# Seven block products instead of eight for 23 pairs of value slabs a layer in a PEER down projection (one core, Trainium2)

## The chip, the cores and the metric

One core of one Trainium2 chip runs the whole kernel. The metric is the time of one execution on the device, in microseconds; lower is better. Names of engines are those of the profile: PE is TensorE (PEld its weight loads), DVE VectorE, ACT ScalarE, POOL GpSimd, SP the queue from which the slabs are fetched.

## What is computed

Two layers of a hybrid decoder over 264 token rows (256 prompt tokens and 8 samples) of width D = 1024. Each layer ends in a PEER feed-forward over 16384 experts, and the change lies in the last part of it, in which the experts' values are summed up:

```python
h = jax.nn.gelu(jnp.einsum('td,ted->te', xb, u_tab[eidx]).astype(F32))
w = (gates * h).astype(xb.dtype)
return jnp.einsum('te,ted->td', w, v_tab[eidx])
```

The kernel computes it densely for the 256 prompt tokens: w is a matrix of 256 tokens by 16384 experts that is zero where an expert was not chosen, and the output is w times the value table of 16384 by 1024, in float32. A layer norm of `alpha * x + output` follows.

## The kernel before, in words

**The stage.** `peer_down` walks through the value table in 128 slabs of 128 experts by 1024 columns (512 KB each). Slab n is multiplied by the block `big[:, n, 0:256]` (128 experts by 256 tokens, the gated activations, which lie in SBUF). There are two blocks of 128 tokens (t) and two halves of 512 columns (g), so four block products for each slab, and each of the four has a PSUM bank of its own (bank 2t + g) in which all 128 slabs are summed.

**The split.** To keep float32 precision, each operand is split in two parts of type fp32r: the high part is a copy with the type fp32r (ACT), and the low part is the difference between the float32 value and the high part (DVE). A block product is three matmuls of 128x128 weights by 512 columns: w_hi by v_hi (L2712), w_lo by v_hi (L2713), w_hi by v_lo (L2714). One slab is 12 matmuls.

**Who does what for one slab.** SP fetches it into one of four ring slots (`refill`, L2565) as soon as the low parts of the slab four before are made. ACT makes `w_hi` (256 columns, L2615) and two halves of `v_hi` (512 columns each, L2616), each when PE has finished the half slab that used the same buffer. DVE makes `w_lo` (L2652) and the two halves of `v_lo` (L2656). PE waits for the low parts. There are two buffers for w and four half buffers for v, so the splitting runs one slab ahead of PE. POOL has no arithmetic in the steady part of this stage.

**The order around it.** The first 32 slabs are written out one by one, since other work is woven in there: the values of the samples' experts are gathered and summed in banks 6 and 7 (`values`, L2724), x is transposed into token rows in bank 5 (L2740), and banks 4 and 6 take the samples' sum (L2731). Slabs 32 to 127 run in loops on ACT, DVE and PE. From slab 32 on the banks 4 to 7 are unused. The last two slabs are multiplied one block of tokens at a time, and then `TokenNorm` begins: DVE adds `alpha * x` to the banks (L2834) and the norm follows.

**Elsewhere.** The up projection before this stage and the dense projections split their slabs in the same way, but there POOL makes the low parts (L2150, and L272 in which POOL and DVE take a half each).

Of the kernel before, what the change touches and what calls it, by code (L numbers as in the profile page):

```python
# [23 lines left out]
F32 = mybir.dt.float32  # L24
# [64 lines left out]
class Step:  # L89


    def __init__(self, nc, io, top):
        self.nc, self.io = nc, io
        self.sb = lambda name, shape, dt=F32, ctx=top: ctx.enter_context(nc.sbuf_tensor(name, shape, dt))


        self.ring, self.ring_lo = self.pair("slab_ring", [P, SLOTS, D], "slab_ring_lo", [P, SLOTS, DC, P])
        self.x = self.sb("x_T", [P, DC, T])
        self.const = self.sb("constants", [P, C_END])
        self.ln = self.sb("ln_scale_shift", [P, LAYERS * 3, 2, DC])  # L100
# [8 lines left out]
        self.later = None  # L109
        self.squares, self.slab_hi = self.pair("squares", [P, DC, T], "slab_hi", [P, 2, DC, P])  # L110
# [76 lines left out]
    def slot_free(self, sp, n):  # L187
# [4 lines left out]
        if kind == "projection":  # L192
            sp.wait_ge(self.product_done, k + 1)
        else:
            sp.wait_ge(self.u_product if kind == "u" else self.v_split, 2 * (k + 1))
# [2302 lines left out]
OWN_AT, VALUES_AT, SUM_FROM, UNROLLED = 10, (12, 18), 22, 32  # L2498


def peer_down(step, layer, block, big, row_index, row_gate, ahead, s_read, s_gated, over):
# [4 lines left out]
    vb = step.slabs[base][1]  # L2506
# [15 lines left out]
    norm = TokenNorm(step, layer, z, small, base + NKEYS if layer + 1 < LAYERS else None)  # L2522
    with ExitStack() as c1:

        got = step.sb("gathered_rows" + L, [P, NB, D], ctx=c1)
# [36 lines left out]
        def _(sp):  # L2562
            def refill(i, s):
                sp.wait_ge(step.v_split, 2 * (vb + SLOTS * i + s + 1 - SLOTS))
                sp.dma_start(step.ring[:, s, :], io["v"][layer * P + SLOTS * i + s]).then_inc(step.slab_ready[s], 16)  # L2565
            for s in range(2):
                refill(1, s)
            sp.wait_ge(s_dense, 1)
            sp.dma_start(step.hidden, dense).then_inc(s_out, 16)
            for s in range(2, SLOTS):  # L2570
                refill(1, s)
            with sp.Fori(2, NKEYS // SLOTS) as i:
                for s in range(SLOTS):
                    refill(i, s)
# [5 lines left out]
        def _(pool):  # L2580
# [23 lines left out]
            norm.gpsimd(pool)  # L2604

        @block.scalar
        def _(act):
            def high(i, s, first):
                n = SLOTS * i + s
                act.wait_ge(step.slab_ready[s], 16 * (base // SLOTS + 1) + 16 * i)  # L2610
                for g in range(2):
                    if not (first and s < 2):
                        act.wait_ge(s_y, 2 * n + g - 3)
                    if g:
                        nc.scalar.activation(wh[:, s % 2, :], big[:, n, 0:TP], ACT.Copy).then_inc(s_wh, 1)  # L2615
                    nc.scalar.activation(hi[:, (2 * s + g) % 4, :], step.ring[:, s, g * HALF:(g + 1) * HALF],  # L2616
                                         ACT.Copy).then_inc(s_hi, 1)
            for n in range(1, UNROLLED):
                high(n // SLOTS, n % SLOTS, n < SLOTS)
# [9 lines left out]
                for r in range(6):  # L2629
                    if n == TOKENS_AT[r] + 1:  # L2630
# [3 lines left out]
                        nc.scalar.activation(z[t][:, g * HALF:(g + 1) * HALF], ps[0:b - a, 5, :], ACT.Copy).then_inc(s_xc, 1)  # L2634
                if n == UNROLLED - 2:
# [3 lines left out]
            with act.Fori(UNROLLED // SLOTS, NKEYS // SLOTS) as i:  # L2639
                for s in range(SLOTS):  # L2640
                    high(i, s, False)
# [3 lines left out]
        def _(dve):  # L2645
            def low(i, s):
                n = SLOTS * i + s
                for g in range(2):

                    if g:  # L2650
                        dve.wait_ge(s_wh, n)
                        nc.vector.tensor_tensor(wl[:, s % 2, :], big[:, n, 0:TP], wh[:, s % 2, :].bitcast(F32),  # L2652
                                                ALU.subtract).then_inc(s_wl, 1)
                    dve.wait_ge(s_hi, 2 * n + g - 1)
                    buf = (2 * s + g) % 4
                    nc.vector.tensor_tensor(lo[:, buf, :], step.ring[:, s, g * HALF:(g + 1) * HALF],  # L2656
                                            hi[:, buf, :].bitcast(F32), ALU.subtract).then_inc(step.v_split, 1)

            for n in range(1, UNROLLED):
                low(n // SLOTS, n % SLOTS)  # L2660
# [12 lines left out]
                if n == SUM_FROM + 5:  # L2673
# [4 lines left out]
                    for g in range(2):  # L2678
                        half = z[2][:, g * HALF:(g + 1) * HALF]
                        link(nc.vector.scalar_tensor_tensor(out=half, in0=half, scalar=ALPHA, in1=ps[0:TS, (4, 6)[g], :],  # L2680
                                                            op0=ALU.mult, op1=ALU.add))
# [3 lines left out]
                if n == UNROLLED - 1:  # L2685
# [3 lines left out]
            with dve.Fori(UNROLLED // SLOTS, NKEYS // SLOTS) as i:  # L2689
                for s in range(SLOTS):  # L2690
                    low(i, s)
# [3 lines left out]
        def _(pe):  # L2695
            def down(i, s, first, final):
                n = SLOTS * i + s
                b = s % 2
                if not first:
                    pe.wait_ge(s_wl, n)  # L2700
                for g in range(2):
                    pe.wait_ge(step.v_split, 2 * (vb + n) + g + 1)
                    buf = (2 * s + g) % 4
# [6 lines left out]
                    for t in range(2):  # L2710
# [3 lines left out]
                        last = nc.tensor.matmul(bank, w_hi[:, ts], v_lo, start=False, stop=final)  # L2714
                    last.then_inc(s_y, 1)

# [25 lines left out]
            for n in range(UNROLLED):  # L2742
                down(n // SLOTS, n % SLOTS, n == 0, False)
# [6 lines left out]
            with pe.Fori(UNROLLED // SLOTS, NKEYS // SLOTS - 1) as i:  # L2750
                for s in range(SLOTS):
                    down(i, s, False, False)
            for s in range(SLOTS - 2):
                down(NKEYS // SLOTS - 1, s, False, False)
            for t in range(2):
                for n in (NKEYS - 2, NKEYS - 1):
                    b = n % 2
                    if t == 0:
                        pe.wait_ge(s_wl, n)
                    for g in range(2):  # L2760
                        if t == 0:
                            pe.wait_ge(step.v_split, 2 * (vb + n) + g + 1)
                        buf = (2 * n + g) % 4
# [14 lines left out]
class TokenNorm:  # L2778
# [46 lines left out]
    def vector(self, dve):  # L2825
# [4 lines left out]
        def residual(t):  # L2830
            for g in range(2):
                dve.wait_ge(self.tile_done, 2 * t + g + 1)
                half = z[t][:, self.halves[g]]
                nc.vector.scalar_tensor_tensor(out=half, in0=half, scalar=ALPHA, in1=step.ps[:, 2 * t + g, :], op0=ALU.mult,  # L2834
                                               op1=ALU.add).then_inc(self.sums, 1)
# [119 lines left out]
    def gpsimd(self, pool):  # L2955
# [5 lines left out]
        split_low(step, pool, self.next_slab + 1, (0, 1))  # L2961
        for c in range(DC // 2):
# [121 lines left out]
```

## Time and profile before

| | |
|---|---|
| Time, median of 3 runs | 2197.09 us (2196.4 to 2197.73) |
| The profiled execution's own time | 2196.69 us |
| Its span, first to last instruction | 2194.9 us |
| PE busy, share of the span | 98% |
| DVE / ACT / POOL busy | 77% / 60% / 46% |
| Matmuls of the down stage (L2712 to L2714) | 3 x 1000 recorded |
| Mean rate of HBM traffic | 186 GB/s |

The rows further down come from the one profiled execution. A row of a timeline gives the start in microseconds from the first instruction, the duration, the engine, the line, the operation and output<-input. An `x2` behind it merges two in a row. PE's matmuls are pipelined, so that their recorded durations (0.39 us) overlap, and the distance from one start to the next is what one costs.

### The profile page before, as it was taken

The numbers are of one execution on the slowest core, as the hardware profiler recorded it, in microseconds if no ns is written. First come the engines' busy times: TensorE is split into PE (matmuls) and PEld (weight loads), VectorE is DVE, ScalarE is ACT, GpSimd is POOL, SyncE is SP. The second block draws the span as 40 slices with busy tenths as digits, with TensorE's granted clock in tenths as the row PEclk, the third lists the DMA queues.
The fourth block names the chain that finished last, engine by engine and source line by source line (L and its number), as shares of the span: only waits on it lengthen the run. The fifth ranks groups of instructions, "written<-read, shape, count | busy, mean of one in ns | idle before, by whom it ended". The sixth has DMA issues, their size and how long they took to land.

```text
span 2194.9 us, 45729 instructions
## 1 busy us (share of the span) xinstructions
PE 2154.5 (98%) x15517; PEld 1961.4 (89%) x15517; DVE 1686.1 (77%) x3908; ACT 1316.4 (60%) x3002; POOL 1014.2 (46%) x820
## 2 busy tenths in 40 slices
PE   8989999999999999999999999999999999999998
PEld 8879799999999877888888988999999998788887
DVE  7766489979999856666656656999799996566666
ACT  6544474557777555555566645645777765555555
POOL 6764447997777610000043344589877774000000
PEclk9999999999999999999999999999999999999999
DMA  7548554554444665555545584455444447555554
GB/s 263 161 143 326 206 179 156 171 176 156 155 159 156 206 218 182 193 194 194 193 164 180 191 362 136 166 168 171 167 155 160 156 147 246 195 192 193 194 195 135
DMA packets 112422, 409.32 MB, mean 186 GB/s; under 512 B 16553, under 2 KB 18769, under 8 KB 107089
## 3 DMA queue, kind: packets, MB, share of 16 engines
q1 hardware_dynamic: 107744, 391.45, 52.2%
q0 software_dynamic: 4528, 15.86, 2.3%
q8 instruction: 95, 1.56, 0.3%
q14 instruction: 55, 0.45, 0.1%
HBM read 397.11 MB, written 10.14 MB: 186 GB/s over the span
## 4 chain that ended last, share of the span: by engine, by line
PE 62%; DVE 16%; POOL 7%; issue 4%; ACT 2%; POOLq 0%; ACTq 0%; DVEq 0%
PE banks L2712 10%; PE banks L2714 10%; PE banks L2713 10%; POOL slab_ring_lo L2150 7%; DVE one_hot_gates L2458 7%; PE banks L2201 5%; PE banks L2202 5%; PE banks L2203 5%; PE banks L296 3%; PE banks L297 3%; PE banks L298 3%; DVE slab_ring_lo L272 2%; DVE expert_activations L2475 2%; PE banks L2223 1%; DVE expert_activations L2466 1%
## 5 line engine op out<-in xcount | busy, mean ns | idle before, releaser
L2150 POOL TENSOR_TENSOR slab_ring_lo<-slab_ring,u_hi 128x512 fp32r<-128x512 f32 x504 | 663.1, 1340 | 167.5 <-ACT u_hi L2255 166.7
L2201 PE MATMUL banks<-operand_hi,u_hi 128*128 128x264 f32 x2016 | 584.8, 290 | 1.6 <-POOL slab_ring_lo L2150 1.6
L2203 PE MATMUL banks<-operand_hi,slab_ring_lo 128*128 128x264 f32 x2048 | 583.3, 285 | 0.0
L2202 PE MATMUL banks<-operand_lo,u_hi 128*128 128x264 f32 x2016 | 573.5, 284 | 0.0
L272 POOL TENSOR_TENSOR slab_ring_lo<-slab_ring,slab_hi 128x512 fp32r<-128x512 f32 x162 | 216.5, 1341 | 593.7 <-ACT slab_hi L262 593.0
L2656 DVE TENSOR_TENSOR v_lo<-slab_ring,v_hi 128x512 fp32r<-128x512 f32 x508 | 350.0, 691 | 117.7 <-ACT v_hi L2616 113.0
L2712 PE MATMUL banks<-v_hi,w_hi 128*128 128x512 f32 x1000 | 391.1, 391 | 3.4 <-DVE w_lo L2652 2.2
L2714 PE MATMUL banks<-v_lo,w_hi 128*128 128x512 f32 x1000 | 389.2, 389 | 0.0
L2713 PE MATMUL banks<-v_hi,w_lo 128*128 128x512 f32 x1000 | 389.2, 389 | 0.0
L2255 ACT ACTIVATE u_hi<-slab_ring 128x512 fp32r<-128x512 f32 x504 | 317.7, 631 | 117.8 <-PE banks L2203 115.2
L2203 PEld LDWEIGHTS banks<-operand_hi,slab_ring_lo 128*128 128x128 f32 x2048 | 385.4, 188 | 0.0
L2201 PEld LDWEIGHTS banks<-operand_hi,u_hi 128*128 128x128 f32 x2016 | 380.7, 189 | 3.3 <-POOL slab_ring_lo L2150 2.5
L2202 PEld LDWEIGHTS banks<-operand_lo,u_hi 128*128 128x128 f32 x2016 | 379.6, 188 | 0.0
L2616 ACT ACTIVATE v_hi<-slab_ring 128x512 fp32r<-128x512 f32 x508 | 316.6, 625 | 85.7 <-PE banks L2714 75.9
L2458 DVE TENSOR_SCALAR one_hot_gates<-banks,squares 128x128 f16<-128x128 f32 x1024 | 336.8, 400 | 0.0
L262 ACT ACTIVATE slab_hi<-slab_ring 128x512 fp32r<-128x512 f32 x288 | 174.4, 626 | 129.5 <-PE banks L298 108.2
L2712 PEld LDWEIGHTS banks<-v_hi,w_hi 128*128 128x128 f32 x1000 | 187.7, 188 | 46.8 <-DVE w_lo L2652 6.4
L2714 PEld LDWEIGHTS banks<-v_lo,w_hi 128*128 128x128 f32 x1000 | 187.7, 188 | 39.3
L2713 PEld LDWEIGHTS banks<-v_hi,w_lo 128*128 128x128 f32 x1000 | 187.8, 188 | 38.5
L2615 ACT ACTIVATE w_hi<-expert_activations 128x256 fp32r (+1 forms) x254 | 106.0, 417 | 177.8 <-PE banks L2714 177.2
L2652 DVE TENSOR_TENSOR w_lo<-expert_activations,w_hi 128x256 fp32r<-128x256 f32 x254 | 107.8, 425 | 133.1 <-ACT w_hi L2615 132.4
L272 DVE TENSOR_TENSOR slab_ring_lo<-slab_ring,slab_hi 128x512 fp32r<-128x512 f32 x126 | 125.3, 995 | 98.4 <-ACT slab_hi L262 98.2
(443 smaller groups left out, 3794.1 us busy)
## 6 DMA issues: line engine op xcount, KB each, us to landing
slab_ring<-in_u SPq DMA_DIRECT2D x256, 512.0 KB
slab_ring<-in_v SPq DMA_DIRECT2D x256, 512.0 KB
slab_ring<-in_proj SPq DMA_DIRECT2D x144, 512.0 KB
cache_k_T<-in_cache_k SPq DMA_DIRECT2D x16, 1024.0 KB, 8.7
cache_v<-in_cache_v SPq DMA_DIRECT2D x16, 1024.0 KB, 11.8
memory_T<-in_mem POOLq DMA_DIRECT2D x2, 1024.0 KB, 6.5
sample_state<-in_state POOLq DMA_DIRECT2D x8, 256.0 KB, 3.9
out_mem_k_out<-mem_k_T SPq DMA_DIRECT2D x16, 128.0 KB, 3.0
```

The source lines that it names most:

```text
L272: (nc.gpsimd if engine is nc.gpsimd else nc.vector).tensor_tensor(step.ring_lo[:, n % SLOTS, cs], step.slab(n)[:, cs], step.slab_hi[:, (k ...
L2150: nc.gpsimd.tensor_tensor(step.ring_lo[:, s, g * HC:(g + 1) * HC, :], step.slab(s)[:, g * HC:(g + 1) * HC, :], part[:, buf].bitcast(F32), ...
L2201: nc.tensor.matmul(bank, part[:, buf, k, :], xh[:, c, :], start=(c == 0), stop=False)
L2202: nc.tensor.matmul(bank, part[:, buf, k, :], xl[:, c, :], start=False, stop=False)
L2203: last = nc.tensor.matmul(bank, step.ring_lo[:, s, c, :], xh[:, c, :], start=False, stop=(c == DC - 1))
L2255: nc.scalar.activation(hi[:, buf], step.slab(s)[:, g * HC:(g + 1) * HC, :], ACT.Copy).then_inc(s_hi, 1)
L2458: last = nc.vector.tensor_scalar(rows[:, g % NB, w, k, :], iota, selT[:, 0, token], gate_parts[:, w, token], ALU.is_equal, ALU.mult)
L2616: nc.scalar.activation(hi[:, (2 * s + g) % 4, :], step.ring[:, s, g * HALF:(g + 1) * HALF], ACT.Copy).then_inc(s_hi, 1)
L2656: nc.vector.tensor_tensor(lo[:, buf, :], step.ring[:, s, g * HALF:(g + 1) * HALF], hi[:, buf, :].bitcast(F32), ALU.subtract).then_inc(step ...
L2712: nc.tensor.matmul(bank, w_hi[:, ts], v_hi, start=first, stop=False)
L2713: nc.tensor.matmul(bank, w_lo[:, ts], v_hi, start=False, stop=False)
L2714: last = nc.tensor.matmul(bank, w_hi[:, ts], v_lo, start=False, stop=final)
```

## The change

Slabs 32 to 123 are taken in 23 groups of four. The first two slabs of a group form a pair; the other two are handled as before ("singles"), and so are slabs 0 to 31 and 124 to 127. The loops are written out.

For a pair, write the weights of slab n as a11 (tokens 0 to 127) and a21 (tokens 128 to 255), those of slab n+1 as a12 and a22, and the two halves of the slabs as b11, b12 (slab n) and b21, b22 (slab n+1). The two by two product of blocks would take eight block products. It is made from seven, by a variant of the scheme of Strassen and Winograd, from sums and differences of the blocks: s3 = a11 - a21, s1 = a22 - a21, s2 = a11 + s1, s4 = a12 - s2, and t1 = b11 + b12, t3 = b12 + b22, t2 = t3 + b11, t4 = t2 + b21.

Products that go to one place only are summed straight into banks 0, 1 and 2 beside the singles; four products that are needed in several places are kept over all 23 pairs in banks 4 to 7 and joined once behind the last pair. Each of the seven is again three matmuls of 128x128 by 512, so a pair is 21 matmuls, not 24.

**Who does what in a group of four slabs.** ACT makes the high parts: of the pair b11 (512 columns), b21 with b22 (1024), t1 with t3 (1024), t2 with t4 (1024), the weights 128, 256 and 512 columns wide, and then the high parts of the two singles as before. DVE makes t1 with t3 (one instruction, 1024 columns), the four weight sums (128 columns each), the low parts of all seven value blocks and of all seven weight blocks, and `w_lo` of the two singles. POOL makes t2 and t4 (512 columns each) and the low parts of the singles' four half slabs, which DVE made before. The value sums and the low parts share their place in SBUF, so that a sum is overwritten by its low part.

SP refills slot 0 and 1 when their low parts and t2, t4 are made. `alpha` is now put on x when the token rows are copied (ACT, scale=ALPHA), so DVE adds without it. Behind the last pair ACT copies one bank, and DVE and POOL together do eight joins of 512 columns, among slabs 124 to 126.

```diff
+PAIRS_FROM, PAIRS_END = 32, 124
+PAIR_PRODUCTS = (("a11", "b11", 4), ("a12", "b21", 0), ("s4", "b22", 1), ("s1", "t1", 5), ("s3", "t3", 7), ("s2", "t2", 6),
+                 ("a22", "t4", 2))
...
+            def sums_of_more(pair):
+
+                pool.wait_ge(s_t13, pair + 1)
+                if pair:
+                    pool.wait_ge(s_q, PER_PAIR * (pair - 1) + 6)
+                nc.gpsimd.tensor_tensor(pair_sum[:, 2, :], pair_sum[:, 1, :], step.ring[:, 0, 0:HALF], ALU.add).then_inc(s_t24, 1)
+                pool.wait_ge(s_t24, 2 * pair + 1)
+                if pair:
+                    pool.wait_ge(s_q, PER_PAIR * pair)
+                nc.gpsimd.tensor_tensor(pair_sum[:, 3, :], pair_sum[:, 2, :], step.ring[:, 1, 0:HALF], ALU.add).then_inc(s_t24, 1)
+
+            def low(n):
+                k = single(n)
+                for g in range(2):
+                    pool.wait_ge(s_hi, 2 * k + g - 1)
+                    buf = (2 * k + g) % 4
+                    nc.gpsimd.tensor_tensor(lo[:, buf, :], step.ring[:, n % SLOTS, g * HALF:(g + 1) * HALF],
+                                            hi[:, buf, :].bitcast(F32), ALU.subtract).then_inc(step.v_split, 1)
+            pool.wait_ge(s_ys, 1)
+            for pair in range(PAIRS):
+                sums_of_more(pair)
...
+                for s in range(2, SLOTS):
+                    low(PAIRS_FROM + SLOTS * pair + s)
...
-            with act.Fori(UNROLLED // SLOTS, NKEYS // SLOTS) as i:
-                for s in range(SLOTS):
-                    high(i, s, False)
+            for pair in range(PAIRS):
+                n = PAIRS_FROM + SLOTS * pair
+                pair_high(pair)
+                high(n + 2)
+                pair_high_last(pair)
+                high(n + 3)
...
+            def pair_low(pair):
+                n = PAIRS_FROM + SLOTS * pair
...
+                pair_v_low(pair, 0, slice(4, 5), step.ring[:, 0, 0:HALF])
+
+                step.wait_slab(dve, base + n + 1)
+                used(pair, 5)
+                halves = step.ring[:, 0:2, :].rearrange("p s (g f) -> p (s g) f", g=2)
+                nc.vector.tensor_tensor(pair_sum[:, two, :], halves[:, 0:4:3, :],
+                                        halves[:, 1:2, :].to_broadcast([P, 2, HALF]), ALU.add).then_inc(s_t13, 1)
+                pair_v_low(pair, 1, slice(5, 7), step.ring[:, 1, :])
+
+                used(pair, 6)
...
+                nc.vector.tensor_tensor(ws[:, 3, :], a11, a21, ALU.subtract)
+                nc.vector.tensor_tensor(ws[:, 4, :], a22, a21, ALU.subtract).then_inc(s_s2, 1)
+                dve.wait_ge(s_s2, 2 * pair + 1)
+                nc.vector.tensor_tensor(ws[:, 5, :], a11, ws[:, 4, :], ALU.add).then_inc(s_s2, 1)
+                dve.wait_ge(s_s2, 2 * pair + 2)
+                nc.vector.tensor_tensor(ws[:, 6, :], a12, ws[:, 5, :], ALU.subtract).then_inc(s_ws, 1)
+                pair_w_low(pair, 0, slice(0, 1), big[:, n, 0:P])
+                pair_w_low(pair, 1, slice(1, 3), big[:, n + 1, 0:TP])
+                dve.wait_ge(s_t24, 2 * pair + 1)
+                pair_v_low(pair, 2, slice(0, 2), sums(slice(0, 2)))
+                pair_w_low(pair, 2, slice(3, PER_PAIR), ws[:, 3:PER_PAIR, :].rearrange("p b f -> p (b f)"))
+                w_low(n + 2)
+                pair_v_low(pair, 3, slice(2, 4), sums(slice(2, 4)))
+                w_low(n + 3)
...
+            def down_pair(pair):
...
+                for w, v, k in PAIR_PRODUCTS:
+                    pe.wait_ge(s_pwl, 3 * pair + w_parts_of[w])
+                    pe.wait_ge(s_pvl, 4 * pair + v_parts_of[v])
...
+                    nc.tensor.matmul(bank, wp[:, 0, a, :], pair_hi[:, b, :], start=(k >= 4 and pair == 0), stop=False)
+                    nc.tensor.matmul(bank, wp[:, 1, a, :], pair_hi[:, b, :], start=False, stop=False)
+                    nc.tensor.matmul(bank, wp[:, 0, a, :], pair_lo[:, b, :], start=False,
+                                     stop=(k >= 4 and pair == PAIRS - 1)).then_inc(s_q, 1)
```

In the products' order, a11 by b11 needs the first low parts of w and v, a12 by b21 the second, the next three (s4, s1, s3) the third ones, and the last two also the fourth of v.

## Rows read from the trace of the kernel before

**Rows 1.** The page: span, and busy shares of the engines.

```profile
span 2194.9 us, 45729 instructions
...
PE 2154.5 (98%) x15517; PEld 1961.4 (89%) x15517; DVE 1686.1 (77%) x3908; ACT 1316.4 (60%) x3002; POOL 1014.2 (46%) x820
```

**Rows 2.** Busy time by stretch: the steady down stage of both layers.

```profile
core 0: us, PE busy (x) PEld busy (x) DVE busy (x) ACT busy (x) POOL busy (x), PEclk, DMA share, GB/s
838.00:1098.00 260.00, 258.88 (x1143) 214.08 (x1142) 173.62 (x293) 151.04 (x287) 0.00 (x0) 1.00 0.59 192
1911.00:2171.00 260.00, 258.88 (x1143) 214.16 (x1142) 173.60 (x293) 151.07 (x287) 0.00 (x0) 1.00 0.58 192
```

**Rows 3.** Timeline of PE in it: the first matmuls of two slabs in a row.

```profile
900.12 0.39 PE L2712 MATMUL banks<-v_hi,w_hi 128*128 128x512 f32 x1
...
902.84 0.39 PE L2712 MATMUL banks<-v_hi,w_hi 128*128 128x512 f32 x1
```

**Rows 4.** Waits, 850 to 1095 us: who for whom, us, times, longest.

```profile
ACT w_hi L2615 <- PE banks L2714: 73.5, 90, 0.8
...
ACT v_hi L2616 <- PE banks L2714: 29.5, 90, 0.3
```

**Rows 5.** Groups by line, 850 to 1095 us: busy us, mean ns | idle before.

```profile
L2656 DVE TENSOR_TENSOR v_lo<-slab_ring,v_hi 128x512 fp32r<-128x512 f32 x181 | 125.4, 693 | 24.5 <-ACT v_hi L2616 24.5
L2616 ACT ACTIVATE v_hi<-slab_ring 128x512 fp32r<-128x512 f32 x180 | 112.7, 626 | 29.5 <-PE banks L2714 29.5
...
L2652 DVE TENSOR_TENSOR w_lo<-expert_activations,w_hi 128x256 fp32r<-128x256 f32 x90 | 38.3, 426 | 58.6 <-ACT w_hi L2615 58.6
L2615 ACT ACTIVATE w_hi<-expert_activations 128x256 fp32r x90 | 37.7, 419 | 73.5 <-PE banks L2714 73.5
```

**Rows 6.** Timeline at 176 us: DVE and POOL on the two halves of a slab.

```profile
175.63 1.29 POOL L272 TENSOR_TENSOR slab_ring_lo<-slab_ring,slab_hi 128x512 fp32r<-128x512 f32 x1 [0.31 <-ACT slab_hi L262]
...
176.14 1.33 DVE L272 TENSOR_TENSOR slab_ring_lo<-slab_ring,slab_hi 128x512 fp32r<-128x512 f32 x1 [0.53 <-ACT slab_hi L262]
```

**Rows 7.** Timelines at 8 and 10 us: the same, each with another one waiting.

```profile
7.79 1.52 POOL L272 TENSOR_TENSOR slab_ring_lo<-slab_ring,slab_hi 128x512 fp32r<-128x512 f32 x1 [7.32 <-ACT slab_hi L262]
...
8.26 1.59 DVE L272 TENSOR_TENSOR slab_ring_lo<-slab_ring,slab_hi 128x512 fp32r<-128x512 f32 x1
...
9.26 1.74 POOL L272 TENSOR_TENSOR slab_ring_lo<-slab_ring,slab_hi 128x512 fp32r<-128x512 f32 x1
...
9.78 1.77 DVE L272 TENSOR_TENSOR slab_ring_lo<-slab_ring,slab_hi 128x512 fp32r<-128x512 f32 x1
```

**Rows 8.** Timelines at 503 and 154 us: DVE with other inputs under POOL.

```profile
503.29 1.30 POOL L2150 TENSOR_TENSOR slab_ring_lo<-slab_ring,u_hi 128x512 fp32r<-128x512 f32 x1 [1.10 <-ACT u_hi L2255]
503.34 0.41 DVE L2458 TENSOR_SCALAR one_hot_gates<-banks,squares 128x128 f16<-128x128 f32 x1
...
503.66 0.95 DVE L2475 TENSOR_TENSOR expert_activations<-squares,expert_activations 128x4 f32<-128x4 f32 x1
...
153.19 1.27 POOL L272 TENSOR_TENSOR slab_ring_lo<-slab_ring,slab_hi 128x512 fp32r<-128x512 f32 x1
...
154.08 0.69 DVE L1620 TENSOR_TENSOR hgrn_out<-banks,exp_cumulative 128x512 f32<-128x512 f32 x1
```

**Rows 9.** Groups by line: busy us, mean ns | idle before; wider instructions.

```profile
L1167 DVE TENSOR_TENSOR operand_lo<-x_T,operand_hi 128x1056 fp32r<-128x1056 f32 x2 | 2.5, 1259 | 5.6 <-ACT operand_hi L1126 5.6
...
L2623 ACT ACTIVATE squares<-expert_activations 128x1024 f32<-128x1024 f32 x1 | 1.1, 1056 | 0.0
```

**Rows 10.** Waits of ACT for transfers of value slabs, whole span.

```profile
ACT v_hi L2616 <- DMA slab_ring<-in_v: 9.0, 5, 3.5
```

**Rows 11.** Timeline at 165 us and two stretches: an idle PE, the granted clock.

```profile
164.93 0.36 PE L296 MATMUL banks<-operand_hi,slab_hi 128*128 128x264 f32 x1 [2.32 <-DVE operand_lo L459]
...
164.00:172.00 8.00, 7.07 (x46) 7.10 (x46) 4.23 (x12) 4.71 (x13) 1.28 (x1) 0.79 0.48 181
88.00:148.00 60.00, 59.19 (x467) 49.36 (x466) 43.67 (x69) 23.53 (x48) 45.66 (x31) 1.00 0.32 104
```

More of the change, by code:

```diff
@@ L2497, with in_pair, single @@
 SAME_PLACE = 512
-OWN_AT, VALUES_AT, SUM_FROM, UNROLLED = 10, (12, 18), 22, 32
+OWN_AT, VALUES_AT, SUM_FROM = 10, (12, 18), 22
+DECODED_STD_AT, DECODED_NORM_AT = 30, 31
+PAIRS_FROM, PAIRS_END = 32, 124
+PAIRS = (PAIRS_END - PAIRS_FROM) // SLOTS
+SINGLES = NKEYS - 2 * PAIRS
+def in_pair(n):
+    return PAIRS_FROM <= n < PAIRS_END and n % SLOTS < 2
+def single(n):
+    assert not in_pair(n)
+    if n < PAIRS_FROM:
+        return n
+    if n >= PAIRS_END:
+        return n - 2 * PAIRS
+    return n - 2 * ((n - PAIRS_FROM) // SLOTS + 1)
+ACT_OF = {"a11": 0, "a12": 1, "a22": 2, "s3": 3, "s1": 4, "s2": 5, "s4": 6}
+VAL_OF = {"t1": 0, "t3": 1, "t2": 2, "t4": 3, "b11": 4, "b21": 5, "b22": 6}
+PAIR_PRODUCTS = (("a11", "b11", 4), ("a12", "b21", 0), ("s4", "b22", 1), ("s1", "t1", 5), ("s3", "t3", 7), ("s2", "t2", 6),
+                 ("a22", "t4", 2))
+PER_PAIR = len(PAIR_PRODUCTS)
 def peer_down(step, layer, block, big, row_index, row_gate, ahead, s_read, s_gated, over):
@@ L2505, in peer_down @@
     base = step.used
-    vb = step.slabs[base][1]
+    vb = layer * SINGLES
     HALF = D // 2
@@ L2562, in _, with refill @@
         def _(sp):
[L2563 to L2567, printed above, removed]
+            def refill(n):
+                before = n - SLOTS
+                if in_pair(before):
+                    pair = (before - PAIRS_FROM) // SLOTS
+                    sp.wait_ge(s_pvl, 4 * pair + 2)
+                    sp.wait_ge(s_t24, 2 * pair + 1 + before % 2)
+                else:
+                    sp.wait_ge(step.v_split, 2 * (vb + single(before) + 1))
+                sp.dma_start(step.ring[:, n % SLOTS, :], io["v"][layer * P + n]).then_inc(step.slab_ready[n % SLOTS], 16)
+            for n in range(SLOTS, SLOTS + 2):
+                refill(n)
             sp.wait_ge(s_dense, 1)
             sp.dma_start(step.hidden, dense).then_inc(s_out, 16)
-            for s in range(2, SLOTS):
-                refill(1, s)
-            with sp.Fori(2, NKEYS // SLOTS) as i:
-                for s in range(SLOTS):
-                    refill(i, s)
+            for n in range(SLOTS + 2, NKEYS):
+                refill(n)
             step.loaded = base + NKEYS
@@ L2606, in _, with high @@
+            pool.wait_ge(s_cv, 2)
+            nc.gpsimd.tensor_tensor(z[1][:, 0:HALF], z[1][:, 0:HALF], pair_sum[:, 0, :], ALU.subtract).then_inc(s_cp, 1)
+            pool.wait_ge(s_cv, 3)
+            for t in range(2):
+                nc.gpsimd.tensor_tensor(z[t][:, HALF:D], z[t][:, HALF:D], pair_sum[:, 1, :], ALU.add).then_inc(s_cp, 1)
+            pool.wait_ge(s_cp, 3)
+            norm.gpsimd(pool, pair_sems)
         @block.scalar
         def _(act):
-            def high(i, s, first):
-                n = SLOTS * i + s
-                act.wait_ge(step.slab_ready[s], 16 * (base // SLOTS + 1) + 16 * i)
+            def high(n):
+                s, k = n % SLOTS, single(n)
+                step.wait_slab(act, base + n)
@@ L2611, in high @@
                 for g in range(2):
-                    if not (first and s < 2):
-                        act.wait_ge(s_y, 2 * n + g - 3)
+                    if k >= 2:
+                        act.wait_ge(s_y, 2 * k + g - 3)
                     if g:
-                        nc.scalar.activation(wh[:, s % 2, :], big[:, n, 0:TP], ACT.Copy).then_inc(s_wh, 1)
-                    nc.scalar.activation(hi[:, (2 * s + g) % 4, :], step.ring[:, s, g * HALF:(g + 1) * HALF],
+                        nc.scalar.activation(wh[:, k % 2, :], big[:, n, 0:TP], ACT.Copy).then_inc(s_wh, 1)
@@ L2620, in _, with pair_high_last @@
+            def pair_high_last(pair):
+                act.wait_ge(s_t24, 2 * pair + 2)
+                nc.scalar.activation(pair_hi[:, 2:4, :].rearrange("p b f -> p (b f)"),
+                                     pair_sum[:, 2:4, :].rearrange("p b f -> p (b f)"), ACT.Copy).then_inc(s_pvh, 1)
+            for n in range(1, PAIRS_FROM):
+                high(n)
                 if n == 1:
@@ L2659, in _, with used @@
-            for n in range(1, UNROLLED):
-                low(n // SLOTS, n % SLOTS)
+                        w_low(n)
+                    dve.wait_ge(s_hi, 2 * k + g - 1)
+                    buf = (2 * k + g) % 4
+                    nc.vector.tensor_tensor(lo[:, buf, :], step.ring[:, n % SLOTS, g * HALF:(g + 1) * HALF],
+                                            hi[:, buf, :].bitcast(F32), ALU.subtract).then_inc(step.v_split, 1)
+            def used(pair, k):
+                if pair:
+                    dve.wait_ge(s_q, PER_PAIR * (pair - 1) + k)
@@ new lines, in pair_low @@
+            def pair_low(pair):
+                n = PAIRS_FROM + SLOTS * pair
+                two = slice(0, 2)
+                sums = lambda blocks: pair_sum[:, blocks, :].rearrange("p b f -> p (b f)")
+                pair_v_low(pair, 0, slice(4, 5), step.ring[:, 0, 0:HALF])
[6 more added lines that the diff above has]
+                used(pair, 6)
+                a11, a21, a12, a22 = (big[:, n + s, t * P:(t + 1) * P] for s in range(2) for t in range(2))
+                nc.vector.tensor_tensor(ws[:, 3, :], a11, a21, ALU.subtract)
[12 more added lines that the diff above has]
+                w_low(n + 3)
@@ L2661, in _ @@
+            for n in range(1, PAIRS_FROM):
+                low(n)
                 if n == 1:
@@ L2741, in token_transposes @@
                 last.then_inc(s_xt, 1)
-            for n in range(UNROLLED):
-                down(n // SLOTS, n % SLOTS, n == 0, False)
+            for n in range(PAIRS_FROM):
+                down(n)
                 if n in VALUES_AT:
```

166 lines of the change are left out of this document (126 added, 40 removed).

## The prediction

> **What bounds the kernel now.** I read the page first. PE is busy for 98% of the span [rows 1]. An average says little about one stage, so I took the stretch that the change touches, the steady part of the down stage in layer 0: PE is busy 258.9 of 260 us at full clock, DVE 173.6, ACT 151.0, and POOL not at all [rows 2]. (Layer 1 shows the same to 0.1 us, so one layer's rows stand for both.) The timeline gives the price of a slab: the first matmuls of two slabs are 2.72 us apart [rows 3]. With 12 matmuls in a slab, one costs 2.72 / 12 = 0.2267 us, and four slabs cost 10.88 us. The waits agree: ACT waits for PE, for a buffer to come free, and none of the view's lines has PE waiting for an operand [rows 4]. So before the change PE is the bound, and each matmul removed is worth 0.2267 us, **as long as nobody else becomes the bound**. That is the question.
>
> **What is removed from PE.** A pair takes 21 matmuls instead of 24. A group of four slabs then has 21 + 24 = 45 matmuls: 45 x 0.2267 = 10.20 us, or 0.68 us less. There are 23 groups in each of two layers, so 46 x 0.68 = 31.3 us less, if PE stays the bound.
>
> **What is added, engine by engine, for one group.** (ACT) Before: eight halves and four w blocks. After: 512 columns six times (b11, the weight sums, four halves of the singles) at 0.626 us [rows 5], 1024 columns three times at 1.06 us [rows 9], 256 columns three times at 0.419 us [rows 5], and 128 columns once, some 0.32 us by the same slope. Together 3.76 + 3.17 + 1.26 + 0.32 = 8.5 us. This fits under 10.2 us.
>
> (DVE) Before: 8 x 0.693 + 4 x 0.426 = 7.25 us. After it has 14 instructions. Four are 1024 wide: 1056 columns took 1.259 us, so I take 1.23 us [rows 9]. Two are 512 wide at 0.693, three 256 wide at 0.426 [rows 5], and five 128 wide. 256 columns more cost 0.267 us, so 128 columns cost 0.426 - 0.133 = 0.293 us. Sum: 4.90 + 1.39 + 1.28 + 1.46 = 9.03 us. Alone, this too fits under 10.2 us, just.
>
> (POOL) Before nothing, after six instructions of 512 columns, two value sums and four low parts of the singles, at 1.29 us [rows 6]: 7.7 us. Alone it fits.
>
> **DVE and POOL together.** Do they run beside each other? The down stage before cannot say, since POOL is silent there. Other stages can. At 175.63 us POOL starts the same kind of subtraction and ends at 176.92. DVE starts its own at 176.14 and ends at 177.47, after 1.33 us instead of 0.69, and 0.55 us after POOL's end, which is about what 512 columns cost without the start [rows 6]. DVE stood still until POOL was through. Where both have the next instruction waiting they take turns: DVE's first ends at 9.85, POOL's second at 11.00, DVE's second at 11.55 [rows 7]. So one POOL and one DVE instruction take 11.55 - 9.85 = 1.70 us, and 1.15 of that is POOL's. It depends on DVE's inputs. At 503.66 a DVE instruction with only four columns, both inputs in SBUF, takes 0.95 us, to the end of the POOL instruction beside it; but the one with an input from a PSUM bank, at 154.08, takes its normal 0.69 us under POOL, and so does one with a single tensor input at 503.34 [rows 8]. All 14 DVE instructions of the new group have two inputs from SBUF, and all six of POOL read SBUF.
>
> The Trainium skill has this as a rule (SBUF — State Buffer, section "Who interferes with whom"): a VectorE instruction with two SBUF inputs and a GpSimd instruction that reads SBUF exclude each other for a whole instruction. By that rule this change, which puts POOL to work beside such instructions, would lose; the rows above agree with it, and the sum below doesn't need it.
>
> **The sum.** Each POOL instruction in the way costs DVE 1.70 - 0.69 = 1.01 us. A group then costs DVE 9.03 + 6 x 1.01 = **15.1 us**, more than PE's 10.2 and than the 10.88 of before. Is there idle time of DVE into which POOL's work could fall? By the waits of the new code, hardly: t1 with t3 waits for the fifth product, the weight sums for the sixth, and PE, which is then ahead of DVE, has both done some 3 us before DVE comes to them. The high parts are ACT's, with 8.5 of 15.1 us. The low parts of t1, t3 wait for POOL's t2, which can start as soon as t1, t3 are there, while DVE still has b21, b22 and the weights to do. So DVE doesn't stop, except under POOL. The stage goes from 10.88 to 15.09 us a group: 46 x 4.21 = 193.7 us more.
>
> Small terms. At the first pair PE has run dry: DVE starts about a slab (2.7 us) before PE has finished slab 31, and needs 4.6 us and a turn of POOL's to the first product's last operand. I take 3 us. The last group saves some 1 us, as PE only has to finish. Joining: ACT's copy and three sums of DVE (0.6 + 3 x 0.69 us) lie beside the 5.4 us of two singles on PE; POOL's three joins block low parts of slabs 124 to 126 three times by 1 us, where DVE has 1.8 us of work in 2.72. I take 1 us. So +3 us a layer, bounds 0 and 8, +6 in all. `alpha` moves into a copy that is there already, and the additions from the banks keep their width: nothing, hidden on an ACT that waits for PE. The ring's refills are SP's as before, 2 MB in 15.1 us instead of 10.88; a slot is freed some 6 us before it is read again, and value slabs were waited for only 5 times in the whole span [rows 10]. Nothing, in the cover of a slower DVE; if this cover were gone, a late slab would cost up to its longest wait, 3.5 us.
>
> Sum against the profiled execution's own 2196.69 us: 2196.7 + 193.7 + 6 = 2396.4. The median of the runs is 0.4 us above it: **2396.8 us**.
>
> **Bounds.** Below: the two only exclude each other while they read, DVE 6528 columns at 0.267 us for 256, 6.8 us, and POOL 6 x 1.15 = 6.9 us, with all starts hidden: 13.7 us a group, 2197 + 130 + 6 = 2333. Above: no start is hidden at all, 9.03 + 6 x 1.29 = 16.8 us, 2197 + 271 + 6 = 2474. The value in between is the one that the alternating rows show directly.
>
> **Rivals.** (1) *PE stays the bound.* If the exclusion doesn't hold for these instructions, or POOL's work falls into gaps of DVE after all so that a group stays at 10.2 us, the time is 2197 - 31 + 6 = 2172, faster. The point from which it decides: DVE's share of a group, with its blocked time, below 10.2 us; that leaves 1.2 us for blocking, one instruction of six. For it: 9.03, 8.5 and 7.7 us fit singly. Against it: rows 6 and 7. Chance 0.06. (2) *Only some of the POOL instructions are in the way*, two or three of six, as with t2 and t4 in a gap: 9.03 + 3 x 1.01 = 12.1 us, 2197 + 56 + 6 = 2259, up to the lower bound. Chance 0.07. (3) *The clock.* PE would work 10.2 of 15.1 us, in pieces with gaps of 1 to 2 us. After a gap of 2.32 us, the granted clock was 0.79 over 8 us, so about 1.7 us of work were lost at the lower of its levels; a 60 us stretch of mixed work kept the full one [rows 11]. Once a group and with nothing to hide it, this is 46 x 1.7 = 78 us on top, 2475; at the low level throughout, a group is 20.4 us of PE work, 2197 + 438 = 2635. Chance 0.06 for more than the bound above. (4) *It doesn't do what it says*: matmuls missing or more than 21 a pair. The loop over seven products is plain; 0.01.
>
> **How the numbers follow.** The forecast with its bounds has 0.80, at 2397. The range is 2325 to 2475, its two bounds and little more; rivals 1, 3 and most of 2 lie outside, some 0.19. A measurement of this kernel can tell 0.2%, 4.4 us. Faster by that: 0.07 (rival 1 and a trifle). Same: 0.01, as only a group of 10.8 to 11.0 us gives it. Slower: 0.92.
>
> **What would show it.** In the changed profile: POOL near 7 to 8 us of each group in the pair stage, its instructions lengthened above 1.29 us; DVE busy over 95% there with its 512-wide ones above 0.69 us, the 128-wide sums above 0.29; waits of PE for DVE's low parts, about 4.9 us a group; pair groups 15.1 us apart; the stage some 98 us longer in each layer, and nothing changed outside it. Wrong would be: PE at 99% with groups of 10.2 us (rival 1), DVE with its old durations beside a busy POOL, PE's clock under 0.95 in the stage (rival 3), or ACT waiting for slabs.

## The result, and the profile after

The changed kernel takes **2366.5 us** (2364.47 to 2369.9, 4 runs), the one before 2197.41 us (4 runs). The ratio is 1.077, with a 95% interval from 1.0751 to 1.0789: slower by 169 us. The forecast was 2397 us in a range from 2325 to 2475.

The page of the changed kernel, against [rows 1]: PE's share has gone from 98 to 92%, DVE's from 77 to 85%, POOL's from 46 to 64%, and DVE now leads the chain that ended last (40% of it, PE 37%; before, PE had 62% and DVE 16%).

```profile
span 2366.4 us, 44081 instructions
...
PE 2171.4 (92%) x15379; PEld 1929.1 (82%) x15379; DVE 2019.2 (85%) x4010; ACT 1369.6 (58%) x3050; POOL 1509.8 (64%) x1102
...
DVE 40%; PE 37%; POOL 7%; issue 7%; ACT 2%; DMA 0%; POOLq 0%; SPq 0%; DVEq 0%; ACTq 0%
```

The busy time in a stretch of the pair stage (columns as in [rows 2]): DVE 268.7 of 270 us, PE 207.4, at full clock. Before, it was PE that was full.

```profile
880.00:1150.00 270.00, 207.44 (x841) 153.12 (x839) 268.69 (x263) 140.76 (x246) 197.64 (x114) 1.00 0.48 145
```

The waits in the same stretch (us in total, times, longest): PE now waits for DVE's low parts, and no line of [rows 4] had PE waiting. DVE itself is in no line as one that waits.

```profile
PEld banks L2919 <- DVE pair_w_parts L2805: 52.8, 38, 1.9
...
PE banks L2919 <- DVE pair_w_parts L2805: 36.6, 38, 1.5
...
PE banks L2919 <- DVE pair_v_lo L2800: 25.5, 18, 1.4
```

One group of four slabs in DVE's timeline:

```profile
1000.95 1.77 DVE L2805 TENSOR_TENSOR pair_w_parts<-pair_w_sums,pair_w_parts 128x512 fp32r<-128x512 f32 x1
1002.63 1.50 DVE L2780 TENSOR_TENSOR w_lo<-expert_activations,w_hi 128x256 fp32r<-128x256 f32 x1
1004.06 2.31 DVE L2800 TENSOR_TENSOR pair_v_lo<-pair_v_sums,pair_v_hi 128x1024 fp32r<-128x1024 f32 x1
1006.30 1.50 DVE L2780 TENSOR_TENSOR w_lo<-expert_activations,w_hi 128x256 fp32r<-128x256 f32 x1
1007.72 0.68 DVE L2800 TENSOR_TENSOR pair_v_lo<-slab_ring,pair_v_hi 128x512 fp32r<-128x512 f32 x1
1008.32 1.21 DVE L2816 TENSOR_TENSOR pair_v_sums<-slab_ring 128x1024 f32<-128x1024 f32 x1
1009.46 1.21 DVE L2800 TENSOR_TENSOR pair_v_lo<-slab_ring,pair_v_hi 128x1024 fp32r<-128x1024 f32 x1
1010.59 1.38 DVE L2822 TENSOR_TENSOR pair_w_sums<-expert_activations 128x128 f32<-128x128 f32 x1
1011.89 0.28 DVE L2823 TENSOR_TENSOR pair_w_sums<-expert_activations 128x128 f32<-128x128 f32 x1
1012.20 1.26 DVE L2825 TENSOR_TENSOR pair_w_sums<-expert_activations,pair_w_sums 128x128 f32<-128x128 f32 x1
1013.50 0.29 DVE L2827 TENSOR_TENSOR pair_w_sums<-expert_activations,pair_w_sums 128x128 f32<-128x128 f32 x1
...
1015.38 1.77 DVE L2805 TENSOR_TENSOR pair_w_parts<-pair_w_sums,pair_w_parts 128x512 fp32r<-128x512 f32 x1
```

and POOL beside it, four low parts of the singles (merged in one row) and the two sums:

```profile
1000.63 6.89 POOL L2680 TENSOR_TENSOR v_lo<-slab_ring,v_hi 128x512 fp32r<-128x512 f32 x4 [1.74 <-ACT v_hi L2708]
1009.61 2.21 POOL L2669 TENSOR_TENSOR pair_v_sums<-pair_v_sums,slab_ring 128x512 f32<-128x512 f32 x1 [2.10 <-DVE pair_v_sums L2816]
1011.90 1.42 POOL L2673 TENSOR_TENSOR pair_v_sums<-pair_v_sums,slab_ring 128x512 f32<-128x512 f32 x1
```

Look at the weight sums. All four are 128 columns wide. Two of them take 0.28 and 0.29 us, and the other two, which meet a POOL instruction, take 1.38 and 1.26 us. The first of these starts at 1010.59 and is through 0.15 us after POOL's end at 1011.82. In the other direction, POOL's sum that starts at 1009.61 takes 2.21 us instead of 1.29, since it has to wait for the 1024-wide subtraction that DVE had begun at 1009.46. Six instructions of the group are stretched in this way, by 1.06 us each on average (1.77 for 0.69, 1.50 for 0.43 twice, 2.31 for 1.22, 1.38 and 1.26 for 0.29), one for each POOL instruction. The subtraction that the timeline begins with comes again in the next group at 1015.38, 14.43 us later; the median over all groups is 14.44 us. Over all 46 groups, 46 x (14.44 - 10.88) = 164 us of the 171.5 by which the span grew; the other 8 are at the edges of the stage, 7.4 of them in two waits of PE, 3.7 us before the first pair of each layer.

### The profile page after: what moved, and what is told of

Read it like the earlier page. It is cut to its first block, busy times and chain, and to the rows that moved or that the text cites. A ratio compares the mean times of both kernels' runs of the same rounds, so it can differ in the third digit from the quotient of the medians.

```text
span 2366.4 us, 44081 instructions
## 1 busy us (share of the span) xinstructions
PE 2171.4 (92%) x15379; PEld 1929.1 (82%) x15379; DVE 2019.2 (85%) x4010; ACT 1369.6 (58%) x3050; POOL 1509.8 (64%) x1102
## 4 chain that ended last, share of the span: by engine, by line
DVE 40%; PE 37%; POOL 7%; issue 7%; ACT 2%; DMA 0%; POOLq 0%; SPq 0%; DVEq 0%; ACTq 0%
DVE pair_v_lo L2800 8%; POOL slab_ring_lo L2153 6%; DVE one_hot_gates L2461 6%; DVE w_lo L2780 6%; PE banks L2204 5%; PE banks L2206 5%; PE banks L2205 5%; DVE pair_w_parts L2805 4%; PE banks L299 3%; PE banks L300 3%; PE banks L301 3%; DVE pair_w_sums L2825 2%; DVE pair_w_sums L2822 2%; DVE pair_v_sums L2816 2%; PE banks L2907 2%
## 5 line engine op out<-in xcount | busy, mean ns | idle before, releaser
L2680 POOL TENSOR_TENSOR v_lo<-slab_ring,v_hi 128x512 fp32r<-128x512 f32 x184 | 317.2, 1753 | 79.6 <-ACT v_hi L2708 79.6
L2919 PE MATMUL banks<-pair_v_hi,pair_w_parts 128*128 128x512 f32 x322 | 142.0, 441 | 155.8 <-DVE pair_w_parts L2805 85.5
L2907 PE MATMUL banks<-v_hi,w_hi 128*128 128x512 f32 x632 | 249.0, 394 | 3.2 <-DVE w_lo L2780 2.2
L2908 PE MATMUL banks<-v_hi,w_lo 128*128 128x512 f32 x632 | 246.8, 391 | 0.0
L2909 PE MATMUL banks<-v_lo,w_hi 128*128 128x512 f32 x632 | 246.7, 390 | 0.0
L2919 PEld LDWEIGHTS banks<-pair_v_hi,pair_w_parts 128*128 128x128 f32 x322 | 61.3, 190 | 222.0 <-DVE pair_w_parts L2805 124.6
L2669 POOL TENSOR_TENSOR pair_v_sums<-pair_v_sums,slab_ring 128x512 f32<-128x512 f32 x46 | 102.1, 2220 | 198.0 <-DVE pair_v_sums L2816 198.0
L2708 ACT ACTIVATE v_hi<-slab_ring 128x512 fp32r<-128x512 f32 x324 | 200.0, 621 | 29.6 <-PE banks L2909 20.0
L2780 DVE TENSOR_TENSOR w_lo<-expert_activations,w_hi 128x256 fp32r<-128x256 f32 x162 | 170.1, 1050 | 9.5 <-ACT w_hi L2707 8.7
L2800 DVE TENSOR_TENSOR pair_v_lo<-pair_v_sums,pair_v_hi 128x1024 fp32r<-128x1024 f32 x92 | 162.3, 1765 | 0.0
```

The costliest lines, as they stand in the source:

```text
L2680: nc.gpsimd.tensor_tensor(lo[:, buf, :], step.ring[:, n % SLOTS, g * HALF:(g + 1) * HALF], hi[:, buf, :].bitcast(F32), ALU.subtract).then_ ...
L2780: nc.vector.tensor_tensor(wl[:, k % 2, :], big[:, n, 0:TP], wh[:, k % 2, :].bitcast(F32), ALU.subtract).then_inc(s_wl, 1)
L2800: nc.vector.tensor_tensor(flat_of(pair_lo), source, flat_of(pair_hi).bitcast(F32), ALU.subtract).then_inc(s_pvl, 1)
L2907: nc.tensor.matmul(bank, w_hi[:, ts], v_hi, start=first, stop=False)
L2908: nc.tensor.matmul(bank, w_lo[:, ts], v_hi, start=False, stop=False)
```

## The experiments

Nine kernels. Each has one run, but for the two kernels of the last part, which have more; four runs of the changed kernel lay within 5.4 us of each other. The median distance between the sums t1, t3 of neighbouring groups in each trace, by which the runs are compared below, is called the length of a group. Where a memset takes the place of a sum or of a low part, that part of the computation is left out.

**Is it POOL's reading?** All six POOL instructions of a group become memsets of the same tiles.

```diff
-                nc.gpsimd.tensor_tensor(pair_sum[:, 2, :], pair_sum[:, 1, :], step.ring[:, 0, 0:HALF], ALU.add).then_inc(s_t24, 1)
+                nc.gpsimd.memset(pair_sum[:, 2, :], 0.0).then_inc(s_t24, 1)
...
-                    nc.gpsimd.tensor_tensor(lo[:, buf, :], step.ring[:, n % SLOTS, g * HALF:(g + 1) * HALF],
-                                            hi[:, buf, :].bitcast(F32), ALU.subtract).then_inc(step.v_split, 1)
+                    nc.gpsimd.memset(lo[:, buf, :].bitcast(F32), 0.0).then_inc(step.v_split, 1)
```

> The six POOL subtractions and additions of a group are memsets of the same tiles (the sums t2, t4 and the singles' low parts are zero): POOL still has an instruction at each place with the same waits and signals, but reads nothing from SBUF. Theory (DVE is held by POOL instructions that read SBUF): DVE's wide instructions go back to 0.69 us for 512 columns, DVE needs 14.44 - 6 x 1.06 = 8.1 us a group, PE is the bound again at 10.2 us, and the time is 2366.5 - 46 x 4.24 = 2171 us, below the kernel before. Rival (DVE is late by its own 14 instructions and the waits between the engines, POOL beside it is harmless): within 20 us of 2366.

Measured: 2174.63 us, 22 us below the kernel before (2196.69 on that chip), and 10.30 us a group. Its windows (columns as in [rows 2]) show PE full, and its groups by line (busy us, mean ns | idle before) show the two DVE instructions that took 1.77 and 1.50 us back at 684 and 418 ns:

```profile
880.00:1080.00 200.00, 200.00 (x876) 163.99 (x875) 159.66 (x272) 145.06 (x255) 62.13 (x118) 1.00 0.64 206
```

```profile
L2779 DVE TENSOR_TENSOR w_lo<-expert_activations,w_hi 128x256 fp32r<-128x256 f32 x40 | 16.7, 418 | 0.0
L2804 DVE TENSOR_TENSOR pair_w_parts<-pair_w_sums,pair_w_parts 128x512 fp32r<-128x512 f32 x20 | 13.7, 684 | 0.0
```

The same program, with the same order and signals, is 192 us faster once POOL reads nothing. (A memset is shorter too, 0.53 us. But it lies under DVE's instructions as the additions did, for instance the one at 901.32 us under those that DVE started at 900.53 and 901.66, and they keep their 1.22 and 0.68 us. Nor is the length of POOL's instruction enough by itself: in [rows 8] a DVE instruction with an input from PSUM keeps its 0.69 us under one of 1.27 us. A memset as long as an addition was not tried.) It also shows what seven products would be worth if nothing stood in their way.

**Is POOL's help worth its price?** All six go to DVE, POOL is idle. Nothing of the computation is left out.

```diff
+                nc.vector.tensor_tensor(pair_sum[:, 2, :], pair_sum[:, 1, :], step.ring[:, 0, 0:HALF], ALU.add).then_inc(s_t24, 1)
...
+                nc.vector.tensor_tensor(pair_sum[:, 3, :], pair_sum[:, 2, :], step.ring[:, 1, 0:HALF], ALU.add).then_inc(s_t24, 1)
...
-                w_low(n + 2)
+                low(n + 2)
                 pair_v_low(pair, 3, slice(2, 4), sums(slice(2, 4)))
-                w_low(n + 3)
+                low(n + 3)
```

> POOL's six instructions a group (t2, t4, the low parts of the singles) are made by DVE, POOL is idle; nothing is left out. Theory: each costs DVE 0.61 us of its own instead of a stop of 1.06 us, so a group takes 14.44 - 6 x (1.06 - 0.61) = 11.7 us and the time is 2366.5 - 46 x 2.7 = 2242 us: taking the help away makes it faster, but not as fast as before the change. Rival (POOL's help is real, DVE alone is overloaded): slower than 2366, up to 2366.5 + 46 x 6 x 0.61 = 2535 us.

Measured: 2233.61 us, 11.50 us a group. Six instructions more on DVE make the kernel 133 us faster, since one of 512 columns costs DVE 0.60 us from start to start when it makes it itself, and 1.06 us of standing still when POOL does.

**One, and four.** The sum t4 alone as a memset; and POOL keeps t2 and t4, DVE makes the low parts of the singles (of the diff of the run before, only the part behind the last `...`).

> Only the sum t4 is a memset instead of an addition, the other five POOL instructions stay (t4 is zero in the products). Theory: one stop of DVE fewer per group, 46 x 1.0 = 46 to 49 us less, 2319 us. Rival (the stops are not each on the path, only their bulk is): less than 15 us changes.

> POOL keeps only t2 and t4, two instructions a group; the four low parts of the singles are made by DVE; nothing is left out. Theory, linear in the POOL instructions: between the all-DVE run (0 of 6, 2233.6 us) and the changed kernel (6 of 6, 2366.5 us), a third of the way: 2278 us. Rival (only the first POOL instruction beside DVE costs, or only the low parts' ones): equal to one of the two ends within 15 us.

Measured: 2326.55 us with 13.49 us a group, 0.95 less than with all six; the weight sum that had met t4 (1.26 us above) is back at 0.29 us, and no other DVE instruction has changed by more than 0.01 us. The 40 us are somewhat less than the 46 to 49 that I expected. The other run: 2276.69 us with 12.45. So 0, 2 and 6 reading instructions give 11.50, 12.45 and 14.44 us: half a microsecond for each, where 1.06 - 0.60 = 0.46 was to be had by the durations.

**Is PE on the path?** An eighth product for each pair, added into bank 3 on top of what belongs there.

```diff
...
+                bank = ps[:, 3, :]
+                nc.tensor.matmul(bank, wp[:, 0, a, :], pair_hi[:, b, :], start=False, stop=False)
+                nc.tensor.matmul(bank, wp[:, 1, a, :], pair_hi[:, b, :], start=False, stop=False)
+                nc.tensor.matmul(bank, wp[:, 0, a, :], pair_lo[:, b, :], start=False, stop=False).then_inc(s_q, 1)
```

> PE makes an eighth block product of three matmuls for each pair (a22 by t4 once more, into bank 3, which makes bank 3 wrong), signalled behind it; 46 x 0.68 = 31.3 us of matmuls more. Theory (DVE is the bound, PE has 4 us of slack a group): 2366 to 2370 us. Rival (PE and the chain of its waits set the time): 2398 us.

Measured: 2368.5 us, 14.47 us a group. 31 us of matmuls put back cost 2 us, no more than two runs of the same kernel differ by. In the changed kernel, the matmuls that Strassen's scheme saves are worth nothing, because they are saved on an engine that waits.

**The cost by itself, without any pair.** The kernel before, with six POOL instructions of 512 columns for every four slabs from slab 32 on, on tiles that nobody uses any more; once additions, once memsets.

```diff
+            for i in range(UNROLLED // SLOTS, NKEYS // SLOTS):
+                pool.wait_ge(step.v_split, 2 * (vb + SLOTS * i))
+                for r in range(6):
...
+                    out = got[:, r // 2, (r % 2) * HALF:(r % 2 + 1) * HALF]
+                    nc.gpsimd.tensor_tensor(out, got[:, 3, 0:HALF], got[:, 3, HALF:D], ALU.add).then_inc(s_x, 1)
```

> The kernel before, without any pair, with six additions of 512 columns on POOL for every four slabs from slab 32 on, from and to tiles that nobody else uses any more; the results stay as they are. Theory: DVE's own work is 8 x 0.61 + 4 x 0.34 = 6.2 us for four slabs, six stops of 1.06 us make it 12.6 us, above PE's 10.88, so the time grows by 48 x 1.7 = 82 us to 2280 us (2250 to 2300, as the six come in a bunch), without any other change. Rival (POOL beside DVE costs only where they share data or waits): 2197 us.

> The same with six memsets of 512 columns on POOL, which write and read nothing. Theory (only a POOL instruction that reads SBUF holds DVE): 2197 us, DVE's 512-wide instructions at 0.69 us. Rival (any POOL instruction holds it): 6 x 0.55 us of stops, 6.2 + 3.3 = 9.5 us, still below 10.88, so the time alone can't tell, but DVE's instructions would be lengthened to over 1 us in part.

Measured: 2317.17 us with the additions, 2197.25 us with the memsets (2194.08 for the kernel before on that chip; single runs). Nothing in POOL's work touches DVE's data, and it costs 120 us. The timeline of the run with additions shows the same turns as [rows 7], DVE and POOL crossing each other:

```profile
1011.47 1.77 DVE L2665 TENSOR_TENSOR v_lo<-slab_ring,v_hi 128x512 fp32r<-128x512 f32 x1
1012.65 1.74 POOL L2612 TENSOR_TENSOR gathered_rows<-gathered_rows 128x512 f32<-128x512 f32 x1
```

With the memsets, DVE's rows are those of [rows 5] to the nanosecond or so, 692 and 426 ns, beside a POOL that is busy 55 of 200 us (groups by line of the run with memsets, columns as above). The memsets lie under DVE's instructions here too, so if POOL's being busy were enough, some of these would be stretched.

```profile
L2665 DVE TENSOR_TENSOR v_lo<-slab_ring,v_hi 128x512 fp32r<-128x512 f32 x148 | 102.5, 692 | 19.9 <-ACT v_hi L2625 19.9
L2661 DVE TENSOR_TENSOR w_lo<-expert_activations,w_hi 128x256 fp32r<-128x256 f32 x74 | 31.5, 426 | 48.2 <-ACT w_hi L2624 48.2
```

The additions cost more than I expected, 2317 us where 2250 to 2300 was the range: four slabs took 13.36 us, not 12.6. My sum had DVE never idle. Here the six came in a bunch, and in 15 such bunches DVE waited 8.1 us for ACT's high parts, 0.54 us for each; ACT had itself waited for buffers that the late PE still used. Where the other 0.2 us went was not followed up.

**A version that uses it.** If the pairs are rarer, DVE can do everything in the time that PE gives it. First a pair in every six slabs, with DVE's and ACT's steps in an order written out by hand:

```diff
-PAIRS_FROM, PAIRS_END = 32, 124
-PAIRS = (PAIRS_END - PAIRS_FROM) // SLOTS
+PAIRS_FROM, PAIRS_END, STRIDE = 32, 122, 6
+PAIRS = (PAIRS_END - PAIRS_FROM) // STRIDE
+DVE_ORDER = (("vl4", 0), ("s3", 0), ("ws1", 1), ("ws2", 1), ("ws3", 1), ("vl1", 1), ("wl1", 1), ("wl2", 1), ("ws4", 1), ("s4", 0), ("t13", 1), ("wl3", 1), ("s5", 0), ("vl2", 1), ("t2", 1), ("t4", 1), ("s2", 1), ("vl3", 1))
...
```

> A pair in every six slabs instead of four (15 pairs and 60 singles a layer from slab 32 to 121), all sums and low parts on DVE, interleaved by hand so that each slab slot of PE has about its own length of DVE work; nothing is left out. Theory: DVE needs 8.1 + 6 x 0.61 = 11.7 us for a pair and two singles and 3.0 us for two singles more, 14.7 us a group; PE needs 21 + 48 matmuls, 15.64 us, so PE is the bound. 30 groups save 0.68 us each, 20.4 us, and run e1 shows that the edges of the pair stage (first pair, joining) cost 9 us for both layers: 2197 - 20 + 9 = 2186 us, faster than the kernel before and after. Rival (the order of waits keeps DVE or PE from being full, ring slots come free too late): 2197 to 2230 us.

Measured: 2208.68 us, ratio to the kernel before 1.0052 (1.0039 to 1.0064). A miss, by the rival's way. From the first pair product of one group to that of the next, PE took 16.1 to 17.3 us and not 15.64. The waits of this kernel between 880 and 1080 us (us in total, times, longest) show who was short: ACT waited for slabs 21 times in 12 groups, DVE for ACT, and PE for DVE.

```profile
ACT v_hi L2684 <- DMA slab_ring<-in_v: 19.8, 11, 2.2
DVE pair_v_lo L2782 <- ACT pair_v_hi L2698: 17.9, 12, 2.9
PEld banks L2925 <- issue: 9.3, 12, 1.2
ACT pair_v_hi L2698 <- DMA slab_ring<-in_v: 7.6, 10, 2.1
...
PE banks L2925 <- DVE pair_v_lo L2782: 4.1, 9, 0.8
```

There are two kinds of these waits for slabs. The smaller part, 7.6 us, is for the first slab of a pair: the pair before it holds two of the four ring slots until its last sums are made, then three slabs are asked for within 2.3 us (948.28 to 950.57 us in one group), and the third of them is that of the next pair. The larger part, 19.8 us, is for the first single behind a pair. Its slot comes free only when DVE, in my order of steps, has made the low parts of the single four slabs before: in the same group SP asked for it at 943.22 us, 5.4 us after the slab before, with next to no transfer under way between 941.2 and 944.2 us (DMA share 0.02), and ACT began to read it at 946.81. On top of this, the first group of a layer took 20.5 and 22.1 us, as the first pair's work stood before PE. So next a pair in every eight slabs, with the first pair's work spread over slabs 27 to 31:

> As the run with a pair in every six slabs, but a pair in every eight (11 pairs a layer, slabs 32 to 119), all sums and low parts on DVE, and the first pair's work is interleaved into slabs 27 to 31 instead of standing before the first product; nothing is left out. Theory: 8.1 + 6 x 0.61 + 4 x 1.5 = 17.7 us of DVE in 21.16 us of PE leaves DVE slack for late slabs, so PE is full: 22 groups save 0.6 us each (45 + 48 matmuls, those of a pair at 0.230 us apart), 13 us, and the edges cost 3 to 6 us: 2198 - 13 + 5 = 2190 us. Rival (the ring of four slots, which a pair holds for longer than a single, starves ACT in every group as it did in the run with six): no faster than the kernel before, 2198 to 2206 us.

Measured: 2193.69 us (11 runs) against 2196.37 (15 runs), ratio **0.9985** (0.9976 to 0.9994). Between 900 and 1100 us PE is busy 199.1 of 200 us (windows, columns as in [rows 2]), and no line of the waits there has ACT waiting for a slab:

```profile
900.00:1100.00 200.00, 199.10 (x873) 163.31 (x872) 173.06 (x294) 125.33 (x230) 4.41 (x3) 1.00 0.63 196
```

This is below the kernel before and the changed one, by 0.15% and 7.3%: the interval lies below 1, but the gain is within the 0.2% that can be told with confidence. Its 22 pairs can save 22 x 0.58 = 13 us at most; some 10 of them are lost. The starts of PE's matmuls in the trace of this run show where. Some four slabs before the first pair, DVE makes weight sums and low parts of that pair ahead of a slab's own low parts, and PE waits for them:

```profile
839.53 0.50 PE L2926 MATMUL banks<-v_hi,w_hi 128*128 128x512 f32 x1 [2.77 <-DVE w_lo L2769]
```

From start to start this gap is 3.16 us, 1.65 more than at the same place before. Behind it, the granted clock is 0.50 (1.2 GHz) from 840.6 to 844.0 us. There the starts are 0.43 us apart and not 0.227, which costs 1.6 us. Two more gaps of 1.2 us, one in the first pair (854.1) and one behind the last pair (1086.0), cost 1.0 us each. Together this is 5.3 us, and layer 1 shows the same gaps and the same clock again.

## Why the prediction was right, step by step

**The side and the mechanism** were right: DVE and POOL exclude each other, and DVE's stops, one for each POOL instruction, take DVE from under PE's time to above it. The forecast read this from [rows 6 to 8], where the stage itself was silent. The runs that remove one, four or all of the readers bear it out, and so does the one that adds six to the kernel before. The rule of the Trainium skill (SBUF — State Buffer, "Who interferes with whom") that a GpSimd instruction which only writes doesn't contend is what the two memset runs show, with DVE at 684 to 692 ns for 512 columns.

**The sum** was 31 us too high: 200 us more were forecast, 169 came. The step that was off is DVE's own work in a group, 9.03 us. The runs show 14.44 - 6 x 1.06 = 8.1 us, and in the run with memsets DVE was busy 159.66 of 200 us, 8.2 us for a group of 10.30. I had added recorded durations. But DVE's records overlap when nothing stands between them: a 512-wide one lasts 0.68 us, and the next starts 0.60 us after it (1007.72 to 1008.32 above); 1024-wide ones start 1.13 us apart and last 1.21. In the group above, twelve of the fourteen instructions start 0.08 us before the one ahead of them is over, and two weight sums start 0.03 us after it: this is the missing 0.9 us. For PE I had taken the distance from start to start, for DVE the duration. In the down stage before, DVE waits so often that the overlap hardly shows, but [rows 7] had it: DVE's second instruction starts at 9.78 us and its first ends at 9.85. The stop itself was 1.06 us for a forecast of 1.01, which makes 0.3 us a group the other way, so that a part of the first error was cancelled by luck. Together, 15.09 against 14.44, and 46 x 0.65 = 30 us.

**No gap of DVE's to hide in**: right, DVE was busy 268.7 of 270 us. **PE's saving is lost**: right, the eighth product costs 2 us. **ACT and the slabs as cover**: right here (ACT 141 of 270 us, three waits for slabs of at most 0.8 us), though the run with six shows how thin the cover of the ring is once DVE is no longer the bound. **PE's saving as such**, 0.68 us a group: 0.58 us in the first run, 10.30 for 10.20 us. All 45 matmuls of a group start 0.2289 us apart on average and not 0.2267: behind each change between pair products and singles, some nine of them are 0.224 to 0.236 us apart, the rest 0.226 to 0.228. The 0.1 us for each pair is also in the run with a pair in eight slabs (21.18 us a group for 93 x 0.2267 = 21.08); its cause is open. **The edges**, +6 us: 8 us, of which 7.4 are PE's wait at the first pair, which had 3 us a layer in the sum. The sum also had three joins of DVE's where the kernel has five, and the profile shows no price for them.

**The rivals.** PE stays the bound at 2172 us: this is what the memset run gave (2174.6 us), so its price was right and its condition false. Only some POOL instructions in the way: all six were. The clock: full in the steady part of the stage. Within the stage it fell only once in each layer, at the first pair: PE stood idle for 3.7 us from 851.5 us on, and from 853.5 to 860.3 us the clock was 0.50, the 1.2 GHz level (2014.0 to 2020.8 us in layer 1). DVE was busy for 6.77 of these 6.80 us, so PE did not set the time there, and no cost of the slower clock shows. The window:

```profile
853.50:860.30 6.80, 4.88 (x11) 3.43 (x12) 6.77 (x8) 5.04 (x10) 5.33 (x4) 0.50 0.53 154
```

## What to carry to other kernels

An idle engine is not free help: before work is moved to POOL, look for a place in the trace where it already runs beside the engine it is to relieve, and see whether one of them gets longer. Here a POOL instruction with SBUF inputs cost a DVE instruction with two SBUF inputs 1.06 us, more than the 0.60 us that DVE would have needed for the same work. And a scheme that saves one of eight block products in exchange for vector work can pay only as often as the vector engine has the time: here a pair in four slabs cost 37 us even with an idle POOL, and a pair in eight gained 0.15%.

For the sum of a full engine, take the distance from one start to the next, not the recorded duration.

## What the runs showed that I had not expected

PE kept its full clock in a stage in which it was busy 77% of the time in pieces with waits up to 1.9 us between them. In this stage it came down only in the one wait of 3.7 us at the first pair of each layer. In the run with a pair in eight slabs, it came down for 3.4 us behind a wait of 2.8 us.

A POOL instruction is stretched as well, the sum t2 to 2.21 us (median) instead of 1.29, but this cost nothing here: between 880 and 1150 us no line of the waits has an engine waiting for POOL.
